# Splitting the combination of y on VectorE, evicting the fourth raw tile earlier and reordering ScalarE's Silus and squares in a hybrid SSD decoder step

## What is computed

```python
z, xbc, dt_raw = split(h @ w_in)                      # gate, x/B/C before the convolution, dt
xbc = silu(causal_depthwise_conv(xbc))                # 4 taps
y_diag = einsum('bcgqs,bcgrqs,bcsgrp', C B^T, decay, x dt)
chunk_states = einsum('bcsgn,bcsgr,bcsgrp', B, decay_to_end, x dt)
h_prev = scan(chunk_states, chunk_decay)              # 4 chunks of 128
y_off  = einsum('bcqgn,bcgrpn,bcqgr', C, h_prev, exp(a_cum))
y = (y_diag + y_off + x * d_skip) * silu(z)
y = rmsnorm_per_group(y) * norm_g                     # 8 groups of 256 features
out = y @ w_out
```

## Time and profile before

| | |
|---|---|
| median of 3 runs | 1620.63 us (1619.62 to 1620.99) |
| profiled execution, its own time | 1624.18 us |
| its span, first to last instruction | 1622.4 us |
| busy in the span: PE | 1516.0 us, 93% |
| DVE | 1161.5 us, 72% |
| ACT | 685.9 us, 42% |
| POOL | 586.5 us, 36% |
| PE clock granted, mean | 0.978 of full speed |

### The profile page before, as it was taken

The page is one execution under the profiler, slowest core; times in us unless marked ns, Lnnn a source line. Parts: engine busy times, 40 slices in busy tenths (PEclk is TensorE's granted clock), DMA queues, the critical chain, the costliest instruction groups (busy, mean ns, idle before and its releaser), DMA issues.

```text
span 1622.4 us, 30561 instructions
## 1 busy us (share of the span) xinstructions
PE 1516.0 (93%) x12329; PEld 1493.6 (92%) x12329; DVE 1161.5 (72%) x1533; ACT 685.9 (42%) x1043; POOL 586.5 (36%) x573
## 2 busy tenths in 40 slices
PE   5898889879996899999999999999999999999996
PEld 5898878879886889999999999999999999999996
DVE  4688888773888788979798454364454897979944
ACT  3755645624556253434343343342234343434321
POOL 3067676641776532324165122200001141404801
PEclk9999999999998999999999999999999999999998
DMA  5444455343443422423324232313222323242311
GB/s 166 109 141 142 133 151 167 127 144 102 137 144 118 139 74 79 131 79 105 105 79 130 79 104 82 102 55 105 79 79 79 105 79 105 79 130 79 126 57 53
DMA packets 158931, 173.44 MB, mean 107 GB/s; under 512 B 13912, under 2 KB 146896, under 8 KB 158784
## 3 DMA queue, kind: packets, MB, share of 16 engines
q1 hardware_dynamic: 137032, 131.30, 25.7%
q0 software_dynamic: 9472, 26.50, 5.2%
q10 hardware_dynamic: 12288, 13.71, 2.9%
HBM read 159.53 MB, written 12.21 MB: 106 GB/s over the span
## 4 chain that ended last, share of the span: by engine, by line
PE 63%; DVE 1%; issue 1%; ACT 1%; POOL 0%; ACTq 0%; DVEq 0%
PE ps L941 28%; PE ps L662 17%; PE ps L966 15%; PE ps L1048 1%; PE ps L682 1%; DVE rstd L1806 0%; PE ps L1016 0%; DVE w_lo L2111 0%; PE ps L919 0%; PE ps L705 0%; POOL ssum L1595 0%; ACT arena L1539 0%; ACT w_hi L1434 0%; PE ps L770 0%; PE ps L1040 0%
## 5 line engine op out<-in xcount | busy, mean ns | idle before, releaser
L662 PE MATMUL ps<-h_hi,w_hi 128*128 128x260 f32 (+2 forms) x1296 | 274.4, 294 | 9.3 <-issue 4.7
L662 PE MATMUL ps<-h_lo,w_hi 128*128 128x260 f32 (+2 forms) x1296 | 265.0, 287 | 0.0
L662 PE MATMUL ps<-h_hi,w_lo 128*128 128x260 f32 (+2 forms) x1296 | 264.3, 286 | 0.0
L1434 ACT ACTIVATE w_hi<-w 128x512 fp32r<-128x512 f32 x232 | 138.2, 626 | 242.6 <-PE ps L941 163.3
L662 PEld LDWEIGHTS ps<-h_hi,w_hi 128*128 128x128 f32 x1296 | 206.1, 193 | 12.5 <-issue 10.3
L941 PE MATMUL ps<-h_hi,w_hi 128*128 128x260 f32 x1024 | 207.2, 284 | 4.7 <-DVE work L2143 4.5
L941 PE MATMUL ps<-h_hi,w_lo 128*128 128x260 f32 x1024 | 207.1, 284 | 0.0
L941 PE MATMUL ps<-h_lo,w_hi 128*128 128x260 f32 x1024 | 206.6, 283 | 0.0
L2111 DVE TENSOR_TENSOR w_lo<-w,w_hi 128x512 fp32r<-128x512 f32 x232 | 188.2, 838 | 25.4 <-ACT w_hi L1434 24.9
L662 PEld LDWEIGHTS ps<-h_lo,w_hi 128*128 128x128 f32 x1296 | 204.9, 193 | 0.0
L662 PEld LDWEIGHTS ps<-h_hi,w_lo 128*128 128x128 f32 x1296 | 204.3, 192 | 0.0
(11 more groups left out here) (259 smaller groups left out, 3592.8 us busy)
## 6 DMA issues: line engine op xcount, KB each, us to landing
w<-in_mlp_w_up SPq DMA_DIRECT2D x32, 1024.0 KB, 5.4
w<-in_mlp_w_down SPq DMA_DIRECT2D x32, 1024.0 KB, 5.2
w<-in_ssd_w_in SPq DMA_DIRECT2D x16, 1024.0 KB, 6.6
w<-in_cm_w_in SPq DMA_DIRECT2D x16, 1024.0 KB, 5.4
w<-in_ssd_w_in SPq DMA_DIRECT2D x16, 512.0 KB, 5.5
arena<-in_state_ssm POOLq DMA_DIRECT2D x64, 128.0 KB, 3.5
arena<-scr_a ACTq DMA_DIRECT2D x16, 512.0 KB, 3.8
arena<-scr_bc POOLq DMA_DIRECT2D x32, 256.0 KB, 3.8
```

What stands on the lines that cost most here:

```text
L662: mm = pe.matmul(ps[:, 2 * slot + b, 0:tn], w[:, pair.w_slot, k, col:col + P], x[:, k, t0:t0 + tn], start=(k == 0 and n == 0), stop=(k == ...
L1434: nc.scalar.activation(blocks(w_hi)[:, (p.ring + n) % 8], src, ACT.Copy)\
```

## The change

Four things move; no instruction is added or taken away.

1. `combine` on DVE is cut in two. `combine_prompt` (the two decay products, then the two sums with the diagonal part) stands ahead of the last convolution and of `sample(g, 3)`. What is left of `combine` behind `sample(g, 3)` is the sample columns and the two gate products.
2. `evac_unit(nxt, 3)`, the eviction of the next group's fourth raw tile, goes from behind `sample(g, 2)` to right behind the chunk states.
3. On ACT the two Silus of x go ahead of the squares of y.
4. `abc_load(g, 0)` on ACT waits for the fourth step of `combine` of the group before (the sums) and no longer for its last gate product, and with the squares moved behind it, it is issued ahead of them.

```diff
@@ ACT, abc_load and window @@
                 if i == 0:
-                    if due(2 * g):
-                        act_e.wait_ge(comb_done, 2 * g)
+                    if due(6 * g - 2):
+                        act_e.wait_ge(cchain, 6 * g - 2)
...
                 exp_m(g, 1)
-                y_squares(g - 1)
                 abc_load(g, 0)
                 silu(g, 2)
                 silu(g, 3)
+                y_squares(g - 1)
                 cst(g)
@@ DVE @@
-            def combine(g):
-
+            def combine_prompt(g):
+
+                n = 6 * g
                 for i in range(2):
-                    n = 3 * (2 * g + i)
                     dve.wait_ge(yoff_done, 2 * g + i + 1)
                     dve.wait_ge(ef_done, 2 * g + i + 1)
                     nc.vector.tensor_tensor(abc[:, 0, i, CH:TP], ps[:, 5 + i, CH:TP], abc[:, 0, i, CH:TP], ALU.mult)\
                       .then_inc(cchain, 1)
-                    if i == 0:
-                        dve.wait_ge(sred_done, 4 * g + 4)
+                for i in range(2):
+                    dve.wait_ge(cchain, n + i + 1)
+                    dve.wait_ge(y1_done, 2 * g + i + 1)
+                    nc.vector.tensor_tensor(work[:, i, CH:TP], work[:, i, CH:TP], abc[:, 0, i, CH:TP], ALU.add)\
+                      .then_inc(cchain, 1)
+
+            def combine(g):
+
+                n = 6 * g + 4
+                dve.wait_ge(sred_done, 4 * g + 4)
+                for i in range(2):
                     nc.vector.scalar_tensor_tensor(out=work[:, i, TP:T], in0=act[:, g % 2, 2 + i, S0:CONV_N:TAPS],
                                                    scalar=dtf[:, 2 * g + i, 16:17], in1=ysmp[:, i, :],
                                                    op0=ALU.mult, op1=ALU.add).then_inc(cchain, 1)
-                    dve.wait_ge(cchain, n + 1)
-                    dve.wait_ge(y1_done, 2 * g + i + 1)
-                    nc.vector.tensor_tensor(work[:, i, CH:TP], work[:, i, CH:TP], abc[:, 0, i, CH:TP], ALU.add)\
-                      .then_inc(cchain, 1)
-                    dve.wait_ge(cchain, n + 3)
+                for i in range(2):
+                    dve.wait_ge(cchain, n + i + 1)
                     dve.wait_ge(z_silu_done, 2 * g + i + 1)
                     nc.vector.tensor_tensor(work[:, i, :], work[:, i, :], zs[:, i, :], ALU.mult)\
                       .then_inc(comb_done, 1)
...
                 states(g)
+                evac_unit(nxt, 3)
                 if more:
                     conv(nxt, 2)
                 sample(g, 2)
-                evac_unit(nxt, 3)
+                combine_prompt(g)
                 if more:
                     conv(nxt, 3)
                 sample(g, 3)
                 combine(g)
```

## The result

The changed kernel takes 1606.07 us (median of 4 runs, 1605.45 to 1607.79), the kernel before 1620.12 us (median of 4, 1618.96 to 1620.99). The ratio is 0.9907, with a 95% interval from 0.9894 to 0.9919: 14.05 us less, inside the range given and 1.8 times the 7.95 us forecast. The profiled execution took 1605.78 us. That of before lay 4 us above its median, so rows set side by side exaggerate: 18.4 us between the two.

The account below looks back on a forecast made before the run. The prediction took a ring through POOL, DVE and ACT as the bound, not PE. Its terms, -13.65 + 4.4 + 1.3 = -7.95 us, took the 1620.63 median to 1612.7 us; range for 8 in 10: 1603.5 to 1618.5.

Parts of the forecast that it names:

- The ring through POOL: POOL's sample states, DVE's last read-out and combine, ACT's squares, POOL's sum of squares: 55.3 us period; PE only hangs on it.
- The short end of the combination: Last read-out's start to POOL's sum of squares: 5.78 to 3.8 us, 1.95 less in seven closings, 13.65 gained.
- The collisions with the fourth pair: DVE's moved sums and convolution meet POOL's fourth pair of sample states: 4.4 us lost, 0.95 or 0.4 a window.
- the slower rival: DVE's two-input instructions and POOL hold each other for whole lengths, 2.5 us more a window: 1625.2 us; 5 in 100.
- also nothing, off the ring: ACT's decay-row load goes out some 8 us earlier; booked as costing nothing.
- the weight's rest meets POOL elsewhere: DVE's weight's rest, 1.55 us earlier against POOL, leaves `y_low` or falls on the first pair's outer products: 1.3 lost.
- in their old distances: DVE's weight's rest, SP's next weight load and POOL's loads all follow 1.95 us earlier, spaced as before.
- the rival without collisions: DVE's sums find POOL idle and `y_low` is freed in windows 1, 4, 6: 1607.0 or 1602.5 us; 23 in 100.
- PE's waits: L781's wait goes; L816 waits about 2 us a window for the masked C B^T; L851 waits longer.
- POOL's period: Time between POOL's sums of squares: to fall from 55.3 to about 54 us, not to 50.

Follow-up runs that it names:

- PE's stall moved away alone: Kernel before with only the two decay products of combine moved ahead of the eviction and the last sample read-out: 1617.81 us, ratio 0.9978.
- 13 us of work added to POOL: Changed kernel with four unused additions on a spare tile behind each of POOL's sums of squares: 1614.75 us, ratio 0.9965.
- the ring opened: Changed kernel with ACT's B and C row copies ahead of the squares, POOL's sum of squares behind those rows' write: 1600.32 us, ratio 0.9869.
- the sums behind the convolution: Changed kernel with the two sums moved behind the fourth convolution, still ahead of the last read-out: 1604.41 us, ratio 0.9907.
- ScalarE's order as before: Changed kernel with ACT's squares put back ahead of the decay-row load and the Silus of x: 1612.83 us, ratio 0.9956.
- the split alone: Kernel before with only combine cut in two; eviction and ACT's order as before: 1612.46 us, ratio 0.995.
- the Silus behind: Changed kernel with the Silus of x behind the squares again, the decay-row load still ahead of both: 1606.7 us, ratio 0.99.
- the three kernels with the split and a late load: Combine cut alone in the kernel before (0.995); changed kernel with squares ahead of load and Silus (0.9956), or load behind Silus and squares (0.9961).
- the load alone: Kernel before with only the decay-row load moved ahead of the squares, waiting for combine's second sum: 1622.96 us, ratio 0.999.

## Why the prediction came out as it did

**The bound was right.** The ring through POOL is shown by three runs: PE's stall moved away alone gave 2.9 us of 32.9, 13 us of work added to POOL cost about 9, and the ring opened gave another 0.4% (0.9869 against 0.9907).

**The short end of the combination: right.** Forecast 1.95 us a closing, seven times, 13.65; measured 40.5 - 26.8 = 13.7.

**The collisions with the fourth pair: somewhat small in sum, wrong in place.** Forecast 4.4 lost. The fourth pair is 41.5 - 38.1 = 3.4 longer in eight windows. In four of them DVE starts the last read-out only 0.5 to 1.3 us behind the pair's end, where before it was there 0.03 behind; that is 2.7 more. Together 6.1, of which 2.5 lie in window 0 alone (the pair 5.38 for 4.15, the read-out 1.3 behind). In windows 1 and 2, where 5.5 to 6 was to be seen, the pair takes 5.16 and 5.17, hardly more than the 5.12 and 5.11 before; only window 6, 5.58, came as forecast. With the sums behind the convolution the pair is as long. That inputs of DVE and POOL side by side cost each other something fits; that the place of the sums decided is not borne out.

How they cost each other can be read from the rows of window 1. POOL's decay starts first, at 169.98, and takes 1.03 us, no more than the 1.04 to 1.11 of the earlier trace rows. The first sum on DVE (the two are read one by one here) starts at 170.34 and ends at 171.44, 0.42 behind the decay's end. POOL's outer product, from 171.15, ends at 171.91, 0.47 behind the end of that sum; the second sum, from 171.36, ends at 172.33, again 0.42 behind the outer product; and so it goes on through the convolution. Whichever starts second waits for what is left of the other's instruction. Before it was the same beside the convolution, whose first instruction ended at 175.74, 0.58 behind the decay. POOL loses 1.1 us by it (its last four instructions take 3.8 us together, 2.7 in window 0 before), and the two sums 0.9. The Trainium skill's page "SBUF — State Buffer", section "Who interferes with whom", says that the shared ports are held for a whole instruction by the one that starts first, and these rows agree with it in full. So the prediction was wrong to read the fourth pair as agreeing "only in part", and the slower rival (1625.2) was wrong in what it made of the rule: it let each instruction pay the other's whole length, 2.5 us more in a window, where only a remainder is paid. The sum of squares agrees as well: 2.59 beside the weight's rest, 1.30 in the run with the ring opened, where it lies clear of it.

**The step that failed: the load that goes out earlier, "also nothing, off the ring", and with it "the weight's rest meets POOL elsewhere", 1.3 lost.** The load itself is off the ring. But POOL's write of the B and C rows, on the ring, comes back late when the weight load is slow (6.1 us where that took 8.7, 4.3 where it took 5.4), and in the run with ScalarE's order as before the weight load was slow with ScalarE's load 2.2 us in front of it, and not 8.2. The prediction let the weight load and POOL's loads follow "in their old distances"; by the split alone ScalarE's load comes 1.3 us behind POOL's loads of sample states and no longer 3.3 (window 1), and the broadcast rises from 29.6 to 33.9. The early load undoes that and more: the broadcast, 28.7, the first pair, 2.2 more, and `y_low`, 4.8 less, make 70.6 against 74.1 before, 3.5 gained where 1.3 lost had been booked. (With the Silus behind, `y_low` and the first pair are about as before and the broadcast shorter still; the time is the same.) A further 1.5 us are gained from the sum of squares to the write (25.7 against 27.2 in seven windows).

So by these rows 13.7 - 6.1 + 3.5 + 1.5 = 12.6 us. Group 4's way to the sum of squares is 0.6 longer and all other pieces of POOL's chain together 2.5 shorter, which makes 14.5 from the fourth pair of window 0 to the last sum of squares, beside 14.05 measured. Of the profiled executions' larger difference, 4.2 us lie ahead of the fourth pair of window 0, 2.5 of them in one wait for a load of sample states (5.17 in before, 2.65 in the changed kernel). The start of window 0's last read-out differs by up to 3.4 us between kernels of this study (122.19 to 125.56), and nothing of it is put down to the change. By times, the load is worth 0.9956 - 0.9907, 0.5% or 8 us; the split alone 8 us as well. The mechanism of the forecast was right and its sum, 7.95, fits the split alone; the term for the load that goes out earlier was booked at nothing and is worth as much again.

That the time lay inside the range owes something to luck. It is within 1 us of the rival without collisions (1607.0), but that rival's sums were to find POOL idle, and they don't: the collisions cost more than forecast, and what made up for them stood in no sum.

**PE's waits: half right.** L781's wait went as foreseen, and L816 took it over, but at 3.9 us a window, not 2, and L851 waits less, not longer. POOL's period fell by 2.5 us, not by 1.3.

**What stays open.** Why the load and the weight slow each other in the split kernels but hardly in before's window 1, at the same distance (129.66 and 131.89 there), was not tried. A candidate from the traces is the pair of sample-state loads that POOL issues behind the fourth pair: before, ScalarE's load goes out 1.9 us behind the end of their issue (126.33 and 1.45 long, then 129.66), with the split and ScalarE's order as before 0.1 ahead of it (125.72 and 1.45, then 127.06). The split moves the one and not the other. The windows sort themselves by it. In the three kernels with the split and a late load, ScalarE's load went out 1.33 us behind the start of this pair in eleven windows, and the broadcast took 4.9 to 6.7 us in ten of them, 4.4 in one; it went out 1.8 behind it in four windows, and the broadcast took 4.3 to 4.6. It cannot be all: before, at the same distances as in window 1, windows 2 and 3 took 5.7 and 5.5. No run moved these loads alone, so this is argued, not shown.

## What to carry to other kernels

When a ring is shortened, what meets in the DMA queues moves with it: a transfer that no instruction of the ring waits for can still slow one that it does wait for, so give each moved DMA a price by the transfers issued within some microseconds of it. A long wait on the busiest engine was here only where the slack showed; to find the ring, look for the chain that returns to its start without that engine. And try the parts of a change in pairs: the split and the early load were worth 8 us each together, and the load alone nothing.

## What the runs showed of the hardware

An 8 KB write from POOL's queue, issued 2.45 us behind a 1 MB load on SP's, came back the later the slower that load was: with ScalarE's order as before it landed at 131.75 + 6.1 = 137.9, the load at 129.29 + 8.7 = 138.0; in the changed kernel 135.0 and 133.6. A part of this can be the write's own queue, where a 128 KB load issued 0.72 us ahead of it landed 0.2 to 0.4 us before it in both. It is not all: in the run with the ring opened, where that load had landed 1.8 to 2.4 us after the write's issue, the write took 2.0 us when issued 0.6 us ahead of the weight load (windows 2 and 3), but 4.2 when issued 0.15 ahead of it (window 1) and 5.2 when issued 0.16 behind it (window 6). The Trainium skill, "DMA: Bandwidth & Descriptors", section "Queues, rings and completion order", says that a DMA engine takes turns between its queues packet by packet, by which one would expect so small a write well before the load's end. Window 1 of that run agrees (4.2 us, the load's end at 6.1), window 6 hardly (5.2, the load's end at 5.5); why is open.

Two sums on DVE with both inputs in SBUF took 1.99 us beside POOL's decay and outer product, 1.81 times their length. The decay, which had started first, was not lengthened at all (1.03), and the outer product, which started behind the first sum, was (0.76 for 0.61). Who pays for such a meeting is the one that starts second, and it pays the rest of the other's instruction.
